# Every second row takes the low weights' product first: matmul order in the projections of an 18-sublayer stack

## The chip, the cores and the metric

The kernel runs on one core of one Trainium2 chip. The metric is the device time of one execution in microseconds (us). A kernel's time is the median of several executions. Differences of about half a per cent are the smallest that such a measurement of this kernel can tell from none.

## The reference

One sequence of 256 tokens with 1024 features passes through two blocks, of four layers and of two. Every layer is: half-weighted feed-forward sublayer, mixer sublayer, half-weighted feed-forward sublayer, each with an RMS norm before and after. That makes 18 sublayers: 12 feed-forward ones and 6 mixers (HGRN twice, differential attention, pooling, a hybrid of Mamba-2 and forgetting attention, RG-LRU). In short:

```python
def swiglu(x, w_in, w_out):
    g, u = jnp.split(x @ w_in, 2, axis=-1)        # 1024 -> 2 x 2816
    return (jax.nn.silu(g) * u) @ w_out           # 2816 -> 1024

for i in range(DEPTH):
    h = h + 0.5 * rmsnorm(swiglu(rmsnorm(h, gn[0]), ffn1_w_in[i], ffn1_w_out[i]), gn[1])
    m = mixer(rmsnorm(h, gn[2]))                  # starts with a projection x @ w_in, ends with one
    h = h + rmsnorm(m, gn[3])
    h = h + 0.5 * rmsnorm(swiglu(rmsnorm(h, gn[4]), ffn2_w_in[i], ffn2_w_out[i]), gn[5])
```

Everything is float32. The work is in the matrix products of the projections, the feed-forward ones above all.

## The kernel before

Activations are kept by feature: a tile has 128 features on the partitions and the 256 tokens (T) along the free dimension, so the 1024 features are KD = 8 rows k of such tiles. Weights come from HBM as panels of 1 MB (`raw`), 256 output columns wide and 8 rows deep; each goes into one of five slots.

**High and low parts.** TensorE multiplies the type fp32r, which is coarser than float32. So every weight panel is split by two engines. ScalarE rounds it to fp32r (`whi`, L1582), and VectorE subtracts (`wlo` = `raw` - `whi`, L1778, in place of `raw`). Activations are split the same way: `xs[:, k, 0:T]` holds the high part of row k and `xs[:, k, T:2T]` the low part beside it; `hs` is the same for the hidden layer of the feed-forward sublayers. A product of weights and activations is then three terms: high weights by high and by low activations, and low weights by high activations.

**One row of a tile's sum.** `tile_product` (L2010) makes the three terms with two matmuls. The high weights (128x128) are multiplied with the 512 columns of `x_k`, so that the first half of a PSUM bank gets high by high and the second half high by low (L2012). The low weights are multiplied with the 256 high columns and added to the first half of the bank (L2013). In this document H is the first kind of matmul (512 columns) and L the second (256 columns), and "a pair" is H and L of one row. Each matmul has a weight load of its own (the rows PEld). A tile of 128 outputs sums 8 rows in one bank: H L H L ..., sixteen matmuls; a panel has two tiles (`ft`). When the panel is done, ScalarE copies the second halves of the banks to `corr` (L1672), and VectorE adds them to the first halves (L1858).

**Where pairs of this kind run.** `in_product` (L2015) calls `tile_product` for the panels of the input projections (`panel_product`, L2079), 20 panels of each feed-forward sublayer and some of each mixer. `down_products` (L2114) calls it for the feed-forward output projection: first seven wide panels with all eight output tiles, two rows k each (L2123), then the last eight rows of every tile, tile by tile (L2133). Some tiles of the output projection use `summed_product` (L2004) in place of it: three matmuls of 256 columns each, high by high, high by low, low by high, all into the same half bank.

**The first two panels** of each sublayer take another path, `first_pair` (L2018): four tiles in turn for each row k, so that TensorE can start as soon as row k of the activations is there. From its second row on it takes the low weights of the four tiles first (L2037), and then the high weights of the four tiles (L2035): L L L L H H H H. The last two rows are made with two tiles at a time: L L H H.

**Order and queues.** Each engine has one program written out by hand, with semaphores between them. TensorE waits once a panel for the split weights (`weights_lo`) and for the banks (`panel_out`), and issues 32 matmuls behind that. The last matmul of a panel raises `panel_done`. Weight DMAs are issued by SyncE's queue, one per panel.

Of the kernel before, what the change touches and what calls it, by code (L numbers as in the profile page):

```python
# [2 lines left out]

# [1 line left out]

# [10 lines left out]
P = 128  # L16
T = 256
TT = T // P
D = 1024
KD = D // P  # L20
FF = 2816
KF = FF // P
PC = 256
SLOTS = 5
# [39 lines left out]
def build(nc, a, out):  # L64
# [9 lines left out]
    for l in range(4):  # L74
        g = VEC_GAIN1 + 6 * l
# [11 lines left out]
    for l in range(2):  # L87
        g = VEC_GAIN2 + 6 * l
# [38 lines left out]
    with ctx:  # L127
        def sb(name, shape, dt=F32):
            return ctx.enter_context(nc.sbuf_tensor(name, shape, dt))
# [3 lines left out]
        def sem(name):  # L133

            if name not in sems:
                sems[name] = ctx.enter_context(nc.semaphore(name))
            return sems[name]
# [5 lines left out]
        wlo = nc.alloc_sbuf_tensor_at("wlo", [P, SLOTS, PANEL], F32R, offset=raw_offset)  # L143
        whi = sb("whi", [P, SLOTS, PANEL], F32R)
# [41 lines left out]
        in_banks = (pp[:, 0:2, :], pp[:, 2:4, :])  # L186
# [1814 lines left out]
        def _(pe):  # L2001
            mm = nc.tensor.matmul
# [4 lines left out]
                mm(bank[:, 0:T], whi[:, slot, c:c + P], x_k[:, T:2 * T], start=False, stop=False)  # L2007
                return mm(bank[:, 0:T], wlo[:, slot, c:c + P], x_k[:, 0:T], start=False, stop=stop)  # L2008

            def tile_product(bank, slot, c, x_k, start, stop):  # L2010

                mm(bank, whi[:, slot, c:c + P], x_k, start=start, stop=False)  # L2012
                return mm(bank[:, 0:T], wlo[:, slot, c:c + P], x_k[:, 0:T], start=False, stop=stop)  # L2013

            def in_product(g, half, ft, x, k):  # L2015
                return tile_product(in_banks[half][:, ft, :], g % SLOTS, k * PC + ft * P, x[:, k, :], k == 0, k == KD - 1)

            def first_pair(seg, fill):  # L2018

# [59 lines left out]
            def panel_product(g, half, between=None):  # L2079
                pe.wait_ge(sem("weights_lo"), splits_before[g] + 1)  # L2080
                for ft in range(2):
                    for k in range(KD):
                        e = in_product(g, half, ft, xs, k)
                    if ft == 0 and between is not None:
                        between()
                e.then_inc(sem("panel_done"), 1)
# [27 lines left out]
            def down_products(s, wide_rows, last_rows, wide_wait, last_wait):  # L2114

                seg = s["segs"][-1]
                for p in range(seg.wide):
                    pe.wait_ge(sem("weights_lo"), splits_before[seg.g0 + p] + 1)
                    wide_wait(p)
                    for ft in range(KD):  # L2120
                        if p == 0 and ft in (4, 6):
                            pe.wait_ge(sem("panel_out"), seg.r0 - (ft == 4))
                        for k in range(2):  # L2123
                            product = summed_product if ft >= KD - 2 else tile_product
                            e = product(out_banks[ft // 2][:, ft % 2, :], (seg.g0 + p) % SLOTS, k * D + ft * P,
                                        hs[:, wide_rows[2 * p + k], :], p + k == 0, False)
                    e.then_inc(sem("panel_done"), 1)
                last_wait()
                for pair in range(4):
                    g = seg.g0 + seg.wide + pair  # L2130
                    pe.wait_ge(sem("weights_lo"), splits_before[g] + 1)
                    for ft in range(2):
                        for k in range(KD):  # L2133
                            product = summed_product if pair == 3 else tile_product
                            e = product(out_banks[pair][:, ft, :], g % SLOTS, k * PC + ft * P, hs[:, last_rows[k], :],
                                        False, k == KD - 1)
                        if pair == 3 and ft == 0:
                            e.then_inc(sem("last_tile_begun"), 1)
                            first_sums(s)
                    e.then_inc(sem("panel_done"), 1)  # L2140
                output_sums(s)
# [19 lines left out]
            def first_sums(s):  # L2161
                pe.wait_ge(sem("squares_added"), 3 * s["n"] + 2)
                mm(psum_stat, ones[:, :], sq[:, 0, :], start=True, stop=False)

            def output_sums(s):

                pe.wait_ge(sem("squares_added"), 3 * s["n"] + 3)
                mm(psum_stat, ones[:, :], sq[:, 4, :], start=False, stop=False)
                pe.wait_ge(sem("last_squares"), 2 * s["n"] + 2)
                mm(psum_stat, ones[:, :], sq[:, 7, :], start=False, stop=True).then_inc(sem("squares_summed"), 1)  # L2170
# [81 lines left out]
            for s in subs:  # L2252
                segs = s["segs"]
                if s["kind"] == FFN:
                    ffn_in(s)
                    f = s["ffn"] * (FF // PC)
                    down_products(s, range(14), range(14, KF), wide_wait=lambda w: pe.wait_ge(sem("hidden_lo"), f + w + 1),
                                  last_wait=lambda: pe.wait_ge(sem("hidden_lo"), f + FF // PC))
                else:
                    last = (out_begin, out_rows, long_out if s["kind"] == HYB else out_rest) if s["kind"] != REC else out_products  # L2260
                    PE_MIX[s["kind"]](pe, s, products, down_products, last, first_of, column_sums, keep_clock)
# [105 lines left out]
```

## Time and profile before

| | |
|---|---|
| median of 3 runs | 3162.26 us |
| lowest and highest | 3154.13 and 3171.62 us |
| span of the profiled execution | 3152.9 us |
| TensorE (PE) busy | 3104.0 us, 98% of the span, 18100 matmuls |
| TensorE weight load (PEld) busy | 2710.0 us, 86% |
| VectorE (DVE) busy | 2183.9 us, 69% |
| ScalarE (ACT) busy | 1681.8 us, 53% |
| GpSimd (POOL) busy | 4.0 us |
| bytes read from HBM | 530.99 MB, 169 GB/s over the span |
| mean granted TensorE clock | 0.998 of full speed |

The span runs from the first to the last instruction of one profiled execution. It is 9.4 us shorter than the median of the runs; that much is taken as what lies around it. PE busy time is the union of matmul intervals whose ends are modelled and overlap, so it tells that TensorE was never without work, not how fast the work went. The rate is read from the distance between the starts of successive matmuls.

### The profile page before, as it was taken

The page shows a single profiled execution, that of the slowest core. Times are in us where ns is not written, and L with a number is a line of the kernel's source. Part 1 is how long each engine was busy: PE and PEld are TensorE (multiplying, and loading weights), DVE is VectorE, ACT ScalarE, POOL GpSimd, SP SyncE. Part 2 cuts the span into 40 slices and gives each one's busy share as a digit, 9 for nine tenths or more (in the row PEclk, how much of TensorE's full clock was granted, in tenths as well). Part 3 has the DMA queues.
Part 4 walks back from the last instruction along what each step waited for, and adds up shares of the span by engine and source line. Part 5 has one row for each costly group of instructions (what it writes and reads, how often), then busy time and mean ns, then how long its engine had stood idle before and what let it go on. Part 6 is the DMA issues. An engine that isn't in the chain of part 4 may idle for free.

```text
span 3152.9 us, 44746 instructions
## 1 busy us (share of the span) xinstructions
PE 3104.0 (98%) x18100; PEld 2710.0 (86%) x18100; DVE 2183.9 (69%) x2635; ACT 1681.8 (53%) x2069; POOL 4.0 (0%) x22
## 2 busy tenths in 40 slices
PE   9999999999999999999999999999999999999998
PEld 8888888888888888888888888888888888888887
DVE  7768675867586775685867877585874675857674
ACT  6566654645464654454546665464642554545553
POOL 0000000000000000000000000000000000000000
PEclk9999999999999999999999999999999999999999
DMA  6543454554355454455454345455432454554453
GB/s 232 188 173 134 149 187 173 190 190 155 120 187 186 175 187 172 149 187 187 174 187 164 131 159 189 161 200 187 162 136 104 161 194 167 198 188 147 147 187 120
DMA packets 75356, 534.78 MB, mean 170 GB/s; under 512 B 8480, under 2 KB 8608, under 8 KB 10784
## 3 DMA queue, kind: packets, MB, share of 16 engines
q1 hardware_dynamic: 75168, 532.07, 46.7%
q8 instruction: 143, 2.34, 0.3%
q14 instruction: 45, 0.37, 0.0%
HBM read 530.99 MB, written 1.05 MB: 169 GB/s over the span
## 4 chain that ended last, share of the span: by engine, by line
PE 92%; DVE 4%; DVEq 2%; ACT 1%; issue 1%; DMA 0%; SPq 0%; ACTq 0%
PE pp L2012 36%; PE pp L2013 18%; PE pm L2012 8%; PE pp L2174 5%; PE pm L2013 4%; PE pp L2035 4%; PE pp L2007 2%; PE pp L2037 2%; PE pp L2006 2%; PE pp L2008 2%; PE pp L2065 2%; PE pp L2217 1%; PE pp L2075 1%; DVE wlo L1778 1%; DMA raw<-weights 0%
## 5 line engine op out<-in xcount | busy, mean ns | idle before, releaser
L2012 PE MATMUL pp<-xs,whi 128*128 128x512 f32 x4592 | 1615.7, 397 | 7.8 <-DVE tsum L1858 7.4
L1778 DVE TENSOR_TENSOR wlo<-raw,whi 128x2048 fp32r<-128x2048 f32 x461 | 1053.8, 2289 | 417.8 <-ACT whi L1582 417.3
L2013 PE MATMUL pp<-xs,wlo 128*128 128x256 f32 x4592 | 1283.2, 279 | 0.0
L2012 PEld LDWEIGHTS pp<-xs,whi 128*128 128x128 f32 x4592 | 861.0, 188 | 219.1 <-DVE tsum L1858 17.3
L1582 ACT ACTIVATE whi<-raw 128x2048 fp32r<-128x2048 f32 x461 | 879.5, 1911 | 281.4 <-DMA raw<-weights 280.7
L2013 PEld LDWEIGHTS pp<-xs,wlo 128*128 128x128 f32 x4592 | 866.1, 189 | 0.6
L1672 ACT ACTIVATE corr<-pp 128x512 f32<-128x512 f32 x335 | 199.5, 595 | 620.9 <-PE pp L2013 595.6
L1858 DVE TENSOR_TENSOR tsum<-pp,corr 128x512 f32<-128x512 f32 x323 | 222.4, 689 | 234.5 <-ACT corr L1672 234.3
L2012 PE MATMUL pm<-hs,whi 128*128 128x512 f32 x1056 | 377.2, 397 | 0.0
L2013 PE MATMUL pm<-hs,wlo 128*128 128x256 f32 x1056 | 296.7, 281 | 0.0
L2012 PEld LDWEIGHTS pm<-hs,whi 128*128 128x128 f32 x1056 | 198.9, 188 | 45.0
L2013 PEld LDWEIGHTS pm<-hs,wlo 128*128 128x128 f32 x1056 | 198.2, 188 | 0.0
L2012 PE MATMUL pp<-hs,whi 128*128 128x512 f32 x528 | 190.8, 397 | 0.0
L2035 PE MATMUL pp<-xs,whi 128*128 128x512 f32 x576 | 166.3, 400 | 16.1 <-DVE xs L1789 16.1
L2006 PE MATMUL pp<-hs,whi 128*128 128x256 f32 x528 | 150.5, 285 | 0.0
L2007 PE MATMUL pp<-hs,whi 128*128 128x256 f32 x528 | 148.4, 281 | 0.0
L2008 PE MATMUL pp<-hs,wlo 128*128 128x256 f32 x528 | 148.4, 281 | 0.0
L2013 PE MATMUL pp<-hs,wlo 128*128 128x256 f32 x528 | 148.4, 281 | 0.0
L1684 ACT ACTIVATE hs<-hid 128x512 fp32r<-128x512 f32 x132 | 83.5, 633 | 108.5 <-DVE hid L1874 108.4
L2174 PE MATMUL pp<-mix,raw 128*128 128x256 f32 x576 | 129.1, 383 | 2.5 <-DVE mix L358 2.5
L2174 PEld LDWEIGHTS pp<-mix,raw 128*128 128x128 f32 x576 | 109.8, 192 | 19.6 <-DVE mix L328 2.9
L2035 PEld LDWEIGHTS pp<-xs,whi 128*128 128x128 f32 x576 | 95.5, 188 | 33.4 <-issue 22.5
(350 smaller groups left out, 3166.2 us busy)
## 6 DMA issues: line engine op xcount, KB each, us to landing
raw<-weights SPq DMA_DIRECT2D x503, 1024.0 KB, 4.8
raw<-weights SPq DMA_DIRECT2D x8, 256.0 KB, 6.9
h<-x_by_feature SPq DMA_DIRECT2D x4, 256.0 KB, 6.2
out<-h SPq DMA_DIRECT2D x4, 256.0 KB, 2.5
vec<-vectors SPq DMA_DIRECT2D x1, 264.0 KB, 2.8
lamrow<-diff_lambda SPq DMA_DIRECT2D x1, 128.0 KB, 11.8
skiprow<-ssm_d SPq DMA_DIRECT2D x1, 8.0 KB, 12.0
```

The lines of the kernel that those rows point to most:

```text
L1582: nc.scalar.activation(whi[:, slot, :], raw[:, slot, :], ACT.Copy).then_inc(sem("weights_hi"), 1)
L1672: nc.scalar.activation(two(corr[:, half, :]), banks[:, :, T:2 * T], ACT.Copy).then_inc(sem("corr_copied"), 1)
L1684: nc.scalar.activation(hs[:, 2 * j:2 * j + 2, 0:T], two(hid[:, :]), ACT.Copy).then_inc(sem("hidden_hi"), 1)
L1778: v.tensor_tensor(wlo[:, slot, :], raw[:, slot, :], whi[:, slot, :].bitcast(F32), ALU.subtract).then_inc(sem("weights_lo"), 1)
L1858: v.tensor_tensor(to, banks[:, :, 0:T], two(corr[:, half, :]), ALU.add).then_inc(sem("panel_out"), 1)
L2006: mm(bank[:, 0:T], whi[:, slot, c:c + P], x_k[:, 0:T], start=start, stop=False)
L2007: mm(bank[:, 0:T], whi[:, slot, c:c + P], x_k[:, T:2 * T], start=False, stop=False)
L2008: return mm(bank[:, 0:T], wlo[:, slot, c:c + P], x_k[:, 0:T], start=False, stop=stop)
L2012: mm(bank, whi[:, slot, c:c + P], x_k, start=start, stop=False)
L2013: return mm(bank[:, 0:T], wlo[:, slot, c:c + P], x_k[:, 0:T], start=False, stop=stop)
L2035: e = mm(bank, whi[:, slot, c:c + P], xs[:, k, :], start=(k == 0), stop=(k == KD - 1))
L2174: return mm(in_banks[p % 2][:, ft, 0:T], raw[:, g % SLOTS, c:c + P], x[:, k, :], start=start, stop=stop)
```

## The change

`tile_product` gets an argument `low_first`. With it, the low weights' matmul is issued first and the high weights' matmul second; the last one issued carries `stop`. It is set for every row with odd k in the input projections, for the second of the two rows of a wide panel, and for odd rows among the last eight of the output projection. The first row of a tile stays high first, since its 512-column matmul opens the whole bank. `summed_product`, `first_pair` and all other matmuls are as before. The order of a tile goes from H L H L H L H L to H L L H H L L H, and since a tile ends with H and the next begins with H, the stream is L L H H L L H H throughout. The number, shapes, operands and results of the matmuls are the same; the terms of each sum are added in another order.

```diff
+from functools import partial
...
-            def tile_product(bank, slot, c, x_k, start, stop):
-
+            def tile_product(bank, slot, c, x_k, start, stop, low_first=False):
+
+                if low_first:
+                    mm(bank[:, 0:T], wlo[:, slot, c:c + P], x_k[:, 0:T], start=False, stop=False)
+                    return mm(bank, whi[:, slot, c:c + P], x_k, start=False, stop=stop)
                 mm(bank, whi[:, slot, c:c + P], x_k, start=start, stop=False)
                 return mm(bank[:, 0:T], wlo[:, slot, c:c + P], x_k[:, 0:T], start=False, stop=stop)
...
-                return tile_product(in_banks[half][:, ft, :], g % SLOTS, k * PC + ft * P, x[:, k, :], k == 0, k == KD - 1)
+                return tile_product(in_banks[half][:, ft, :], g % SLOTS, k * PC + ft * P, x[:, k, :], k == 0, k == KD - 1, k % 2 == 1)
...
-                            product = summed_product if ft >= KD - 2 else tile_product
+                            product = summed_product if ft >= KD - 2 else partial(tile_product, low_first=k == 1)
...
-                            product = summed_product if pair == 3 else tile_product
+                            product = summed_product if pair == 3 else partial(tile_product, low_first=k % 2 == 1)
```

## Rows read from the trace of the kernel before

**Rows 1.** The page: engines and clock, then the chain that ended last, by line.
```profile
PE 3104.0 (98%) x18100; PEld 2710.0 (86%) x18100; DVE 2183.9 (69%) x2635; ACT 1681.8 (53%) x2069; POOL 4.0 (0%) x22
...
PEclk9999999999999999999999999999999999999999
...
PE 92%; DVE 4%; DVEq 2%; ACT 1%; issue 1%; DMA 0%; SPq 0%; ACTq 0%
PE pp L2012 36%; PE pp L2013 18%; PE pm L2012 8%; PE pp L2174 5%; PE pm L2013 4%; PE pp L2035 4%; PE pp L2007 2%; PE pp L2037 2%; PE pp L2006 2%; PE pp L2008 2%; PE pp L2065 2%; PE pp L2217 1%; PE pp L2075 1%; DVE wlo L1778 1%; DMA raw<-weights 0%
```
**Rows 2.** PE's waits: engine, line, waited for: us in total, times, longest.
```profile
PE pp L2035 <- DVE xs L1789: 16.1, 17, 1.0
PE pp L2012 <- DVE tsum L1858: 7.4, 8, 2.1
```
**Rows 3.** Groups by line: operation, tiles, shapes, count | busy us, mean ns | idle before.
```profile
L2012 PE MATMUL pp<-xs,whi 128*128 128x512 f32 x4592 | 1615.7, 397 | 7.8 <-DVE tsum L1858 7.4
L2012 PE MATMUL pm<-hs,whi 128*128 128x512 f32 x1056 | 377.2, 397 | 0.0
L2012 PE MATMUL pp<-hs,whi 128*128 128x512 f32 x528 | 190.8, 397 | 0.0
```
**Rows 4.** L2012 alone, 90 us of feed-forward inputs: us, busy (count), clock, DMA, GB/s.
```profile
31.00:121.00 90.00, 90.00 (x260) 48.63 (x260) 1.00 0.53 194
372.00:462.00 90.00, 90.00 (x256) 47.91 (x255) 1.00 0.51 185
...
2975.00:3065.00 90.00, 90.00 (x256) 47.92 (x255) 1.00 0.52 185
```
**Rows 5.** L2012 alone between the starts of two of its matmuls, first stage.
```profile
39.58:118.62 79.04, 79.04 (x229) 42.75 (x229) 1.00 0.52 188
```
**Rows 6.** Timeline of PE, first feed-forward stage: start us, us, line, operation.
```profile
39.93 0.39 PE L2012 MATMUL pp<-xs,whi 128*128 128x512 f32 x1
40.16 0.27 PE L2013 MATMUL pp<-xs,wlo 128*128 128x256 f32 x1
40.27 0.40 PE L2012 MATMUL pp<-xs,whi 128*128 128x512 f32 x1
...
40.97 0.40 PE L2012 MATMUL pp<-xs,whi 128*128 128x512 f32 x1
```
**Rows 7.** Timeline of PE, second feed-forward sublayer's input stage.
```profile
382.01 0.40 PE L2012 MATMUL pp<-xs,whi 128*128 128x512 f32 x1
...
384.13 0.40 PE L2012 MATMUL pp<-xs,whi 128*128 128x512 f32 x1
```
**Rows 8.** Timeline of PE, output projection: pairs, then the three 256-column matmuls.
```profile
145.17 0.40 PE L2012 MATMUL pm<-hs,whi 128*128 128x512 f32 x1
...
147.29 0.40 PE L2012 MATMUL pm<-hs,whi 128*128 128x512 f32 x1
...
149.06 0.28 PE L2006 MATMUL pp<-hs,whi 128*128 128x256 f32 x1
...
149.41 0.28 PE L2006 MATMUL pp<-hs,whi 128*128 128x256 f32 x1
```
**Rows 9.** Timeline of PE, first_pair of a feed-forward sublayer, LLLLHHHH and then LLHH.
```profile
547.23 1.08 PE L2035 MATMUL pp<-xs,whi 128*128 128x512 f32 x4
...
548.62 1.09 PE L2035 MATMUL pp<-xs,whi 128*128 128x512 f32 x4
...
551.43 1.09 PE L2035 MATMUL pp<-xs,whi 128*128 128x512 f32 x4
552.36 0.40 PE L2037 MATMUL pp<-xs,wlo 128*128 128x256 f32 x2
552.60 0.63 PE L2035 MATMUL pp<-xs,whi 128*128 128x512 f32 x2
553.06 0.40 PE L2037 MATMUL pp<-xs,wlo 128*128 128x256 f32 x2
...
554.46 0.39 PE L2037 MATMUL pp<-xs,wlo 128*128 128x256 f32 x2
```

## The prediction

> **What bounds the kernel now.** I read the page first. TensorE is busy for 98% of the span, its granted clock is 9 tenths or more in every slice, which is its 2.4 GHz level, and the chain of work that ended last lies for 92% on TensorE; lines 2012 and 2013, the two that the change reorders, hold 66% of the span in it (36 + 18 + 8 + 4) [rows 1]. Then the waits: TensorE's longest total against one releaser is 16.1 us, in `first_pair`, which the change leaves alone, and the next is 7.4 us [rows 2]. So nothing that TensorE waits for is worth much; what counts is how fast it streams one matmul after another.
>
> How fast is not in the mean durations, since their ends are modelled: the mean of 397 ns for H [rows 3] is longer than the distance from one H to the next. I take starts. In the first feed-forward stage H begins at 39.93, its L at 40.16 and the next H at 40.27: about 230 ns for H, 115 for L; three pairs take 1.04 us [rows 6]. Over a long stretch it is exact: 229 starts of L2012 from 39.58 to 118.62, so 228 pairs in 79.04 us, 346.7 ns a pair [rows 5]. In the next feed-forward sublayer six pairs take 384.13 - 382.01 = 2.12 us, 353.3 ns a pair [rows 7]. Nothing in the code differs between the two. Windows of 90 us in all twelve feed-forward input stages show just these two rates: 260 or 261 starts in eight of them, 256 in four [rows 4]. I call them the quick rhythm and the slow rhythm. In the output projection six pairs take 147.29 - 145.17 = 2.12 us, the slow rhythm again, and there three matmuls of 256 columns take 149.41 - 149.06 = 0.35 us [rows 8]. That last row matters: H and L are 768 columns with two weight loads, the three are 768 columns with three weight loads and no 512-column matmul among them, and both take 353 ns. Time goes by columns, not by the number of loads or by what stands next to what.
>
> **What the change removes, adds and moves.** It removes and adds no matmul, load, wait or transfer. It reorders the two matmuls in every second row. The pairs are 4592 + 1056 + 528 = 6176 [rows 3]; half of them, 3088, are turned round, and the stream becomes L L H H. Nobody is released earlier or later within a tile: the last matmul of a panel is now H, which starts 115 ns sooner than L did, and ends when L ended, since the same columns stand before that point. The waits on `weights_lo`, `panel_out` and `hidden_lo` stand ahead of the first matmul of a panel and keep their place, and SP's queue isn't touched. So the whole question is what a pair costs in the order L L H H.
>
> The trace of before shows that very order, in the last two rows of `first_pair`. There the blocks L L H H begin at 552.36, 553.06, with two more up to 554.46: three blocks, six pairs, in 2.10 us, 350 ns a pair. Its middle rows, L L L L H H H H, begin an H block at 547.23 and at 551.43, three turns of four pairs later: 4.20 / 12 = 350 ns again [rows 9]. Two L together took 0.24 us and two H 0.46 us. So 350 ns is my price. It differs from the stream at hand in one way: there neighbours of one kind share the activations of one row, here they don't. The ends around it are the two rhythms, 346.7 and 353.3 ns.
>
> The sum, in terms of pairs:
> - eight quick feed-forward stages, 20 panels of 16 pairs each: 8 x 320 = 2560 pairs, from 346.7 to 350, +3.3 ns each: +8.5 us (0 to +17.1 between the ends);
> - four slow stages, 4 x 320 = 1280 pairs, from 353.3 to 350: -4.3 us (-8.5 to 0);
> - the mixers' projections, 4592 - 3840 = 752 pairs, in short stretches that I put at the middle of the two rates: 0 (-2.5 to +2.5);
> - the output projections, 1056 + 528 = 1584 pairs at 353.3. Two different makeups took the same time there, which speaks for 0; the price of 350 would give -5.3 us, the quick rhythm -10.5. I take half of the former: -2.6 us.
>
> Together +8.5 - 4.3 + 0 - 2.6 = +1.6 us on a span of 3152.9. The median of the runs is 9.4 us above that span, and I carry this over: 3162.26 + 1.6 = 3164 us. The ends are 0 - 8.5 - 2.5 - 10.5 = -21.5 us, all in the quick rhythm, and +17.1 + 2.5 = +19.6 us, all in the slow one. The three runs of before lie 17.5 us apart, which is what eight stages cost between the rhythms (17.1 us); the trace of one execution can't show whether that is the cause.
>
> A rule of the Trainium skill bears on this. First the row: L lasts some 115 ns from start to start and holds the load for the next matmul under it, and an L that follows an L costs no visible excess, 0.24 us for two [rows 9]. "TensorE: Matmul & The Clock Gate", section "LDWEIGHTS (loading the stationary operand)", gives a load of 128 columns as P / 1.2, 107 ns, and its section on the back-to-back gap gives 109 ns for a warm matmul of 256 columns. By that rule a load just fits under an L in either order, and the sum would be zero; but it leaves 2 ns of slack, so a load only slightly slower would make L L the bad order. The same section's gaps for 512 and 256 columns add to 325 ns for a pair; the trace disagrees, with 346.7 and 353.3.
>
> **The rivals.**
> *All quick (faster).* Alternating H and L might be what throws the stream into the slow rhythm: each H is followed by something of another length. If blocks of two of a kind keep it quick everywhere, the time is 3162.26 - 21.5 = 3141 us, -0.7%. For it: the switch between the rhythms has no visible cause in the code, so it hangs on something as small as order. Against it: the L L H H of `first_pair` took 350 and not 346.7.
> *Uncovered load (slower).* While H streams, the queue has 115 ns to spare beside the load of L. If that slack is now used to get ahead with the load after it, then in L L H H the second L has no such stock, and its load sticks out. The place is the matmul behind the first L of each block. The dearest that the rows allow there is what two L took above twice 115: 0.24 - 0.23 = 0.01 us, give or take as much for the two decimals, so 0 to 20 ns; it decides from about 5 ns, where 3088 x 5 = 15 us. At a middle 7 ns it gives 3088 x 7 = 21.6 us, 3184 us. Against it: three loads under three 256-column matmuls cost no more than two loads in a pair [rows 8].
> *All slow.* If blocks of unlike activations lose the quick rhythm for good, the price is +19.6 us, 3182 us. Its nearest row is the 353.3 of the slow stages.
> *The change does nothing.* The array might be bound by columns alone, with the rhythm set by how each stage starts. The time is then 3162 us, with stages falling into one or the other as they do now.
>
> **How the numbers follow.** My forecast of 3164 us, with prices of 348 to 352 ns, has 0.45; that the order does nothing, 0.13; all quick 0.20; all slow 0.10; uncovered load 0.12. Half a per cent is 16 us, about what a measurement of this kernel can tell from no change. The first two lie within it: 0.58. All quick is faster: 0.20. All slow and uncovered load are slower: 0.22. The range runs from the bound of all quick, a little beyond it at 3139, to 3184, the middle of the uncovered load, and leaves out the rest of both: gains from blocks that beat even the quick rhythm, and loads that stick out by 10 ns or more. The likeliest case's own range is 3152 to 3172.
>
> **What the profile after would show.** The count of L2012's successor in 90 us windows of the twelve stages: near 258 in all if my price is right, 260 or 261 if all are quick, 256 if all are slow, under 253 if loads stick out. Starts: blocks of 0.70 us; the second L of a block at 0.12 us behind the first, and more than that if its load is uncovered. The waits of TensorE should stay within some 2 us of [rows 2]. I am wrong if the output projection's pairs move by more than 4 ns from 353, or if any block takes less than 0.69 us: then the order of unlike matmuls has a price of its own, which I have put at nearly nothing.

## The result

The changed kernel takes 3139.87 us (median of 4, 3139.15 to 3141.14), the kernel before 3162.74 us beside it (median of 4, 3154.13 to 3171.62). The ratio is 0.9923, 95% interval 0.9902 to 0.9943: faster by 0.8%, where 3164 us and no change beyond half a per cent had been forecast. Two things stand out. The time is within 2 us of the rival "all quick" (3141 us), though the trace does not bear its mechanism out in the input stages. And the executions of the changed kernel lie within 2 us of each other, where those of the kernel before were 17.5 us apart.

The page after, with the lines that answer to [rows 1], then TensorE's two longest waits by releaser, as in [rows 2]:

```profile
PE 3089.7 (98%) x18100; PEld 2700.5 (86%) x18100; DVE 2185.3 (70%) x2635; ACT 1681.6 (54%) x2069; POOL 4.1 (0%) x22
...
PE 91%; DVE 5%; DVEq 2%; ACT 1%; issue 1%; DMA 0%; POOL 0%; POOLq 0%; ACTq 0%; SPq 0%
...
PE pp L2039 <- DVE xs L1790: 16.2, 17, 1.0
PE pp L2016 <- DVE tsum L1859: 6.9, 7, 2.1
```

The waits are the same to 0.5 us, VectorE and ScalarE work as long as before, and TensorE's busy time is 14.3 us shorter, just as the span is (3138.6 against 3152.9 us). The gain lies in the stream itself.

To compare rates I take windows that begin just behind the start of one matmul and end as far behind the start of the matmul 224 pairs later, in the dense part of an input stage; the columns are stretch, its length, busy (count of matmuls that read `xs`), granted clock, share of the DMA engines, GB/s. First the kernel before, stages 1, 2 and 12 of the twelve:

```profile
36.51:114.17 77.66, 77.66 (x450) 1.00 0.52 190
377.82:456.96 79.14, 79.14 (x450) 1.00 0.50 185
...
2980.51:3059.65 79.14, 79.14 (x450) 1.00 0.52 186
```

Then the changed kernel, the same three:

```profile
36.89:114.91 78.02, 78.02 (x450) 1.00 0.54 189
377.46:455.49 78.03, 78.03 (x450) 1.00 0.54 189
...
2968.84:3046.86 78.02, 78.02 (x450) 1.00 0.53 189
```

Before: 77.66 / 224 = 346.7 ns a pair in eight stages and 79.14 / 224 = 353.3 ns in four. After: 78.02 / 224 = 348.3 ns in all twelve, a new rate between the two, not the quick one. The same view for the last rows of the output projection, over 40 pairs, with `hs`; first before, then after:

```profile
173.14:187.27 14.13, 14.13 (x82) 1.00 0.55 176
```

```profile
173.40:187.26 13.86, 13.86 (x82) 1.00 0.50 183
```

That is 353.3 ns a pair before and 346.5 ns after, in all twelve output projections. Since 13.86 us is read to 0.01, the rate after lies between 346.3 and 346.7; by the trace's whole nanoseconds, two pairs begin 693 or 694 ns behind the two before once the stretch is under way, and that is 346.7 ns, the quick rhythm. The timeline of the changed kernel shows how the new order runs there (start us, us, line; L2016 and L2015 are H of even and odd rows, L2017 and L2014 their L), to be held against [rows 8]:

```profile
145.95 0.40 PE L2016 MATMUL pm<-hs,whi 128*128 128x512 f32 x1
146.19 0.28 PE L2017 MATMUL pm<-hs,wlo 128*128 128x256 f32 x1
146.31 0.28 PE L2014 MATMUL pm<-hs,wlo 128*128 128x256 f32 x1
146.42 0.39 PE L2015 MATMUL pm<-hs,whi 128*128 128x512 f32 x1
146.65 0.40 PE L2016 MATMUL pm<-hs,whi 128*128 128x512 f32 x1
```

An H behind which another H waits takes 0.23 us to the next start, one behind which an L waits takes 0.24, and the second L of the two takes 0.11, the first 0.12. The block H L L H takes 0.69 us (2 x 346.5 ns) where two pairs took 0.71.

The account between the two profiled executions: the output projections give 1584 x (353.3 - 346.5) = 10.8 us; the eight quick input stages lose 2560 x (348.3 - 346.7) = 4.1 us; the four at the slow rhythm give 1280 x (353.3 - 348.3) = 6.4 us. Together 13.1 of the 14.3 us; the other 1.2 us are left to the mixers' 752 pairs, and start to start over every such pair of the two traces the mixers' do come out 1.3 us shorter. The medians moved by more, 22.9 us. The difference is in the kernel before: the profiled execution of the changed kernel took 3140.28 us as a run, 1.7 us above its span, so 1.7 and not 9.4 us lie around a span. The profiled execution of before took 3152.9 + 1.7 = 3154.6 us by that, one of the faster ones of its kernel, whose median of the first four executions stands 8 us above it. In 46 later executions of the kernel before, beside the experiments, the median is 3157 to 3158 us, so part of the 22.9 us is that the first four came out high; five more executions of the changed kernel, beside 17 of those, are 16.8 us faster.

### The profile page after: what moved, and what is told of

Same layout as the page of the kernel before. It is cut to its first block, busy times and chain, and to the rows that moved or that the text cites. A ratio compares the mean times of both kernels' runs of the same rounds, so it can differ in the third digit from the quotient of the medians.

```text
span 3138.6 us, 44746 instructions
## 1 busy us (share of the span) xinstructions
PE 3089.7 (98%) x18100; PEld 2700.5 (86%) x18100; DVE 2185.3 (70%) x2635; ACT 1681.6 (54%) x2069; POOL 4.1 (0%) x22
## 4 chain that ended last, share of the span: by engine, by line
PE 91%; DVE 5%; DVEq 2%; ACT 1%; issue 1%; DMA 0%; POOL 0%; POOLq 0%; ACTq 0%; SPq 0%
PE pp L2016 18%; PE pp L2015 18%; PE pp L2017 9%; PE pp L2014 9%; PE pp L2178 5%; PE pp L2039 4%; PE pm L2016 4%; PE pm L2015 4%; PE pp L2041 2%; PE pm L2017 2%; PE pp L2009 2%; PE pp L2007 2%; PE pm L2014 2%; PE pp L2008 2%; PE pp L2069 2%; PE pp L2221 1%
## 5 line engine op out<-in xcount | busy, mean ns | idle before, releaser
L2016 PE MATMUL pp<-xs,whi 128*128 128x512 f32 x2296 | 916.2, 399 | 7.2 <-DVE tsum L1859 6.9
L2015 PE MATMUL pp<-xs,whi 128*128 128x512 f32 x2296 | 908.3, 396 | 0.0
L2014 PE MATMUL pp<-xs,wlo 128*128 128x256 f32 x2296 | 639.2, 278 | 0.0
L2017 PE MATMUL pp<-xs,wlo 128*128 128x256 f32 x2296 | 636.9, 277 | 0.0
L2014 PEld LDWEIGHTS pp<-xs,wlo 128*128 128x128 f32 x2296 | 431.0, 188 | 104.8
L2017 PEld LDWEIGHTS pp<-xs,wlo 128*128 128x128 f32 x2296 | 431.8, 188 | 96.6
L2016 PEld LDWEIGHTS pp<-xs,whi 128*128 128x128 f32 x2296 | 435.9, 190 | 19.4 <-DVE tsum L1859 16.8
L2015 PEld LDWEIGHTS pp<-xs,whi 128*128 128x128 f32 x2296 | 430.3, 187 | 0.0
L2016 PE MATMUL pm<-hs,whi 128*128 128x512 f32 x528 | 209.6, 397 | 0.0
L2015 PE MATMUL pm<-hs,whi 128*128 128x512 f32 x528 | 205.0, 388 | 0.0
L2039 PE MATMUL pp<-xs,whi 128*128 128x512 f32 x576 | 166.2, 400 | 16.2 <-DVE xs L1790 16.2
L2017 PE MATMUL pm<-hs,wlo 128*128 128x256 f32 x528 | 148.2, 281 | 0.0
L2009 PE MATMUL pp<-hs,wlo 128*128 128x256 f32 x528 | 147.9, 280 | 0.0
L2014 PE MATMUL pm<-hs,wlo 128*128 128x256 f32 x528 | 145.9, 276 | 0.0
```

Of the source, the lines that this page charges most:

```text
L2015: return mm(bank, whi[:, slot, c:c + P], x_k, start=False, stop=stop)
L2039: e = mm(bank, whi[:, slot, c:c + P], xs[:, k, :], start=(k == 0), stop=(k == KD - 1))
```

## The experiments

The theory after the result, called A: the stream of matmuls has its own price for each order, H L H L falls by chance into one of two rhythms in every input stage of every execution, and H L L H has one rhythm only. Against it stood B: the two halves of the change work on each other, the rhythm of one stage being handed to the next. The place of the operands in SBUF, the traffic of other engines and the weight loads were the suspects for where the price comes from.

### The change in the output projections only

```diff
-                return tile_product(..., k == 0, k == KD - 1, k % 2 == 1)
+                return tile_product(..., k == 0, k == KD - 1)
```

> The new order only in the output projections (`down_products`); the input projections keep H L H L. Theory A (each order has a price of its own, and the H L stream of the input stages falls by chance into a quick or a slow rhythm in each execution): the output projections give 1584 pairs x 7.3 ns = 11.5 us, so the median is near 3151 us against 3162 us for the kernel before, and the scatter between executions (17 us in the kernel before) stays, since it comes from the input stages. In the profile, twelve input stages at 346.7 or 353.6 ns a pair. Theory B (the change as a whole keeps the stream quick, since a slow output projection throws the next sublayer's stages out of step): all input stages are quick here too, the scatter is gone, and the time is near 3136 us.

Measured: 3145.12 us (median of 12, 3140.41 to 3154.58), ratio 0.9956 (0.9935 to 0.9977) to the kernel before, whose 29 executions beside it have a median of 3158.05 us. The input stages kept both rates; here stages 2 and 3:

```profile
376.38:454.03 77.65, 77.65 (x449) 1.00 0.54 189
565.74:644.88 79.14, 79.14 (x449) 1.00 0.53 186
```

Five of the twelve are slow in this execution, and the scatter stayed (14 us). So making the output projections quick doesn't make the input stages quick, and B falls in this form. The gain of 12.9 us is near the 10.8 us of the account and the 11.5 us of theory A. Of the 29 executions of the kernel before, 28 lie within 10.4 us; the other, at a mean granted clock of 0.935 where they had 0.997 to 0.999, took 3193.53 us.

### The change in the input projections only

```diff
-                            product = summed_product if ft >= KD - 2 else partial(tile_product, low_first=k == 1)
+                            product = summed_product if ft >= KD - 2 else tile_product
...
-                            product = summed_product if pair == 3 else partial(tile_product, low_first=k % 2 == 1)
+                            product = summed_product if pair == 3 else tile_product
```

> The new order only in the input projections; the output projections keep H L H L. Theory A: all twelve input stages at 348.4 ns a pair, the scatter between executions falls from 17 us to about 2 us, the output projections stay at 353.4 ns, and the median is 11.5 us above that of the changed kernel, near 3151 us. Theory B: the input stages, entered from slow output projections, show two rates from stage to stage, and the scatter stays.

Measured: 3151.70 us (median of 12, 3149.68 to 3153.53), ratio 0.9973 (0.9953 to 0.9993). All twelve input stages run at 78.02 / 224 = 348.3 ns and all output projections at 353.4 ns; the scatter is 3.9 us. Both are as A expected, the scatter somewhat wider than its 2 us.

### Both halves again

No edit: the changed kernel.

> The changed kernel itself, beside the kernels of this call on the same chip, as the sum of the two halves. If the halves add up (output projections alone 0.9956, input projections alone 0.9973 of the kernel before), it is at 0.9929 of the kernel before, and its executions lie within 3 us of each other. If the halves overlap, it is above 0.994.

Measured: 3140.12 us (median of 5, 3137.42 to 3140.47), ratio 0.9942 (0.9927 to 0.9956) to 17 executions of the kernel before with a median of 3156.90 us. The two halves together, 0.9956 x 0.9973 = 0.9929, lie within that interval, at its edge. The ratio itself is just above 0.994, where the expectation had put an overlap. So this run can't tell halves that add up from a small overlap; that they add up is told by the rates, which are the same in each half alone and in both together (348.3 ns and 346.5 ns). The gain is somewhat smaller than in the first comparison since the kernel before came out at 3157 to 3158 us here, and at 3163 us in its first four executions.

### The kernel before, two more executions with a profile

> The kernel before, unchanged, in another execution with a profile: does the number of slow input stages tell its time? In the profile of before four of twelve were slow (353.8 against 346.6 ns a pair, 2.3 us a stage). If the rhythm is the cause of the scatter, an execution with n slow stages takes about 3154 + 2.3 x (n - 4) us, give or take 2 us for the mixers' stages, which have rhythms too. If the scatter has another cause, time and count don't go together.

> The same once more: another execution of the kernel before, with 3154 + 2.3 x (n - 4) us for n slow input stages if the rhythm makes the scatter.

Measured: 3146.73 us with one slow stage of twelve (the second), 3152.14 us with four (the first four); forecast by the rule, 3147.1 and 3154. Stages 1 and 2 of the first execution, then stages 4 and 5 of the second:

```profile
36.77:114.42 77.65, 77.65 (x450) 1.00 0.53 189
378.18:457.32 79.14, 79.14 (x450) 1.00 0.52 187
```

```profile
891.13:970.27 79.14, 79.14 (x450) 1.00 0.52 186
1083.12:1160.77 77.65, 77.65 (x450) 1.00 0.53 189
```

The same program, bit for bit, has its stages in another rhythm in each execution, and between these two the time follows their number: three more slow stages cost 5.4 us, that is 1.8 us each, where 320 x (353.3 - 346.7) = 2.1 us are due. Start to start in the traces, the twelve input stages differ by 6.3 us, which is 2.1 for each of the three; the rest of the execution gave 0.9 us back. The earlier profiled execution had four stages in the slow rhythm too and a span 2.5 us longer than this one with four (3152.9 against 3150.4 us), so something besides varies as well. It isn't the mixers' pairs, which took 1.2 us less there. Some 1.7 us of it are one stretch of another matmul, L390, near the end: first the earlier execution, where the granted clock was 0.59 from 2892 to 2896 us, then this one:

```profile
2892.16 4.54 PE L390 MATMUL pm<-mix,raw 128*128 128x256 f32 x12 [1.70 <-DVE small L298]
```

```profile
2893.53 2.86 PE L390 MATMUL pm<-mix,raw 128*128 128x256 f32 x12 [1.70 <-DVE small L298]
```

From 3146.7 us with one slow stage, a median of 3158 us would have six or seven slow stages at 2.1 or 1.8 us each. That is an estimate: no execution near the median has a profile, and neither have the slowest ones.

### TensorE alone

A kernel of its own, which loads three weight panels and the input and then does nothing but run streams of matmuls, 12 tiles of 8 rows each. It leaves out the whole computation of the reference. One of its streams:

```diff
+            for n in range(4):
+                mm(pm[:, 3, 0:240 if n == 3 else T], ones[:, :], keep[:, 0:240 if n == 3 else T], start=True, stop=True)
+            for tile in range(12):
+                for i, (w, k) in enumerate(orders("HL")):
+                    bank, lhs, rhs = place(tile, w, k, "lo", 0, False)
+                    mm(bank, lhs, rhs, start=(i == 0), stop=(i == len(orders("HL")) - 1))
```

> Nothing of the reference is computed: the output is zeros. After loading three weight panels and the input, TensorE alone runs 25 streams, each of 96 pairs (12 tiles of 8 rows) or what the order makes of them, with no transfer and no other engine at work; 3 matmuls of 256 columns and one shorter or equal one of type float32 stand between streams, to shift the start. Orders: H L; H L L H; runs of 4 and of 8 of a kind; H alone; L alone; three 256-column matmuls per row; low first in every row; the weights of L taken from `whi`; one row of activations only; one weight address only; each with the activations at a multiple of 128 bytes, some also 16, 32 and 64 bytes past it. Theory A (price of an order, rhythm by start): H L at 0 bytes shows 346.7 and 353.4 ns in its four starts, H L L H 348.4 ns at each start and 346 ns at 64 bytes. Theory C (the excess over 325 ns, and the two rhythms, come from the other engines' and the DMAs' traffic in SBUF): all streams run near 325 ns, whatever the order. Theory D (the address of the weights decides): the streams with one weight address or one weight source differ from the others by several ns a pair.

The windows run over the 72 rows from the third tile to the eleventh, with the same columns as above. In this order: H L at 0 bytes with a 256-column start, and with a 240-column start; H L at 64 bytes, both starts; H L L H at 0 bytes; H L L H at 64 bytes; three matmuls of 256 columns at 0 bytes, and at 64 bytes.

```profile
29.21:54.65 25.44, 25.44 (x146) 1.00 0.00 1
64.73:89.69 24.96, 24.96 (x146) 1.00 0.00 1
169.49:194.61 25.12, 25.12 (x147) 1.00 0.01 1
204.74:230.18 25.44, 25.44 (x146) 1.00 0.00 1
240.33:265.41 25.08, 25.08 (x146) 1.00 0.00 1
310.53:335.37 24.84, 24.84 (x146) 1.00 0.00 1
547.39:573.31 25.92, 25.92 (x218) 1.00 0.01 1
583.57:609.01 25.44, 25.44 (x218) 1.00 0.01 1
```

Per row: H L at 0 bytes 353.3 and 346.7 ns, H L at 64 bytes 348.9 and 353.3, H L L H 348.3 at 0 bytes and 345.0 at 64, the three matmuls 360.0 at 0 bytes and 353.3 at 64. With no transfer under way and no other engine at work, the rates of the real kernel are there to the tenth of a nanosecond: 346.7, 353.3 and 348.3 ns in the input stages, 353.3 in the old output projections and for their three-matmul tiles. One isn't: the new output projections run at 346.5 to 346.7 ns, and the stream like them at 345.0; no run shows why. Theory C is refuted: the rhythms are there with TensorE alone. The output projections of the kernel before are the streams at 64 bytes: `hs` begins 64 bytes past a multiple of 128, `xs` at a multiple.

The other streams: runs of four of a kind 350.8 ns and of eight 349.2 ns at 0 bytes, and of eight 344.9 ns at 64 bytes, so more neighbours of one kind don't help; low first in every row 349.9 ns, mostly an alternation again; L reading its weights from `whi`, one row of activations only, or one weight address only, 346.7 ns each, a rate that H L shows anyway, so none of these is needed for it. With one stream each, they can't settle theory D. H alone took 226.7 ns and L alone 120.0 ns, together 346.7.

### More starts and more places

The same kernel with other streams.

> Nothing of the reference is computed: the output is zeros. Streams on TensorE alone, as in the streams before, 12 tiles of 8 rows each. Eight streams of H L with the activations at a multiple of 128 bytes that differ only in the length of the float32 matmul ahead of them (256, 256, 240, 208, 176, 144, 112, 80 columns); one behind a stream of 256-column matmuls; three starts of H L at 64 bytes; H L L H at 0, 16, 32, 48, 64, 80, 96 and 112 bytes and at other starts; three 256-column matmuls per row at 0, 16, 32 and 64 bytes; the same with every second row turned round. Theory A with the rhythm set by the start: H L falls to 346.7 or to 353 ns from start to start, and H L L H has one rate at each place, 348.4 at 0 and 345.0 at 64 bytes, whatever stands ahead. If the rhythm is not set by the start, all eight streams of H L agree. The three 256-column matmuls should take 360 ns a row at 0 bytes and 353.4 at 64.

In this order: H L at 0 bytes, twice with the same 256-column start; three matmuls of 256 columns at 0 bytes; H L at 64 bytes; H L L H at 0, and at 64 bytes.

```profile
29.27:54.23 24.96, 24.96 (x146) 1.00 0.00 1
64.37:89.81 25.44, 25.44 (x146) 1.00 0.00 1
312.52:338.44 25.92, 25.92 (x218) 1.00 0.01 1
454.85:480.29 25.44, 25.44 (x146) 1.00 0.01 1
525.84:550.92 25.08, 25.08 (x146) 1.00 0.00 1
666.48:691.32 24.84, 24.84 (x146) 1.00 0.00 1
```

The first two streams are the same instructions, and one is quick, the other slow. Of the eight starts of H L at 0 bytes six were slow (353.3) and two quick (346.7), and a ninth, behind the stream of three matmuls, was quick; in the kernel of streams above, one of four was slow. The first stream of both kernels is the same, with the same matmuls ahead, and was slow there and quick here. H L at 64 bytes was slow in all three starts. H L L H gave 348.3 ns in both starts at 0 bytes and 345.0 in all three at 64 bytes. Other places: 348.3 at 16 bytes, 346.7 at 32, 350.0 at 48, 80 and 96, 348.9 at 112. Turning every second row of the three-matmul form round changed nothing (360.0 and 353.3). The expectation held on each point. So the length of the matmul ahead does not decide the rhythm.

### The weight load's share

> Nothing of the reference is computed: the output is zeros. Streams on TensorE alone again. The weights are 128, 64 or 32 columns wide, so that their load is shorter; the moving columns stay 512 and 256. The weights' address is moved by 32 and by 64 bytes with the activations at 0 and at 64. H L has four starts each with the activations at 32 and at 16 bytes. Theory X (the excess over 325 ns a pair comes from the weight load, which shares something with the moving operand): with half the load it halves or vanishes, and the weights' address matters as much as the activations' does. Theory M (the excess is in reading the moving operand alone): 348.4 and 345.0 ns for H L L H at 0 and 64 bytes whatever the width and the address of the weights.

With weights of 64 columns in place of 128, H L took 340.0 ns at 0 bytes and 343.3 at 64; with 32 columns 348.3 at both. H L L H took 350.0 and 347.8 ns with 64 columns, 346.7 and 350.0 with 32. The excess that theory X has in mind doesn't halve with half the load, and with a quarter of it is as large as ever, against theory X; but it doesn't stay put either, against theory M. The weights' address counts as well: moved by 64 bytes together with the activations (both at 64), H L L H took some 349 ns in place of 345.0 (moved by 32 bytes, 351.5 with the activations at 0 and 347.2 at 64), and the three-matmul form with the weights alone moved took 353.8 in place of 360.0. (One row in sixteen, at the panel's end, kept its weights' place.) So the places of both operands matter. It isn't their distance alone: with the weights moved by 64 bytes and the activations at 0, H L L H took 347.9 ns, not the 345.0 of the opposite case. The windows, again over 72 rows: H L L H with the weights moved, the activations at 0 and at 64; the three-matmul form with the weights moved; H L with weights of 64 columns at 0 bytes.

```profile
557.37:582.42 25.05, 25.05 (x145) 1.00 0.00 1
592.53:617.64 25.11, 25.11 (x145) 1.00 0.00 1
627.63:653.10 25.47, 25.47 (x218) 1.00 0.01 1
273.89:298.37 24.48, 24.48 (x145) 1.00 0.00 1
```

H L with the activations at 16 or 32 bytes was quick in all four starts each. How load and moving operand meet in the engine stays open.

### Moving the activations of the kernel before

```diff
+        sb("mix_pad", [P, 16])
         mix_offset = nc.sbuf_base
...
```

> The kernel before with 64 bytes of padding ahead of `mix` and `hs`, so that `hs` begins at a multiple of 128 bytes as `xs` does; in the kernel before it begins 64 bytes past one. No order is changed. Theory A1 (the slow 353.4 ns of the output projections comes from where their activations lie in SBUF): they go to the two rates of the input stages, 346.7 ns where they are quick, and the median falls by up to 1584 x 6.7 = 10.6 us, to about 3152 us. Theory A2 (place has nothing to do with it, order alone has a price): the output projections stay at 353.4 ns and the time stays at 3162 us within the scatter.

Measured: 3148.73 us (median of 12, 3145.60 to 3151.02), ratio 0.9964 (0.9944 to 0.9984). The time fell by 9.3 us, which A2 had not said. The median is near what A1 said, and its reason is wrong: the output projections stayed at 353.3 ns, as A2 said, and it was the input stages that were quick, all twelve of them in the profiled execution. The three-matmul tiles went from 0.35 to 0.36 us a row, as in the streams at 0 bytes. Why the input stages should be quick more often when `hs`, which they don't read, is moved, no run shows. That what comes ahead of a stage sways its rhythm is a guess; the order of the rows in the output projection did not. But the odds of the two rhythms are not the same in every layout, and "by chance" in theory A has to be read with that.

Next, `xs` of the kernel before is moved by 64 bytes:

```diff
+        sb("xs_pad", [P, 16])
...
         xs = sb("xs", [P, KD, 2 * T], F32R)
+        sb("after_pad", [P, 16])
```

> The kernel before with `xs` moved by 64 bytes in the same way; the order stays H L H L. Theory A: the input stages run at the two rates that H L showed 64 bytes past a multiple of 128, 348.9 and 353.1 ns, in place of 346.7 and 353.8 ns. The sum for each stage of 320 pairs is between +0.7 us (quick to quick) and -0.2 us (slow to slow), so the median stays within 6 us of the kernel before, and the scatter between executions shrinks from 17 us, since the two rates lie closer together. Theory A2: stages at 346.7 and 353.8 ns as before.

Measured: 3166.03 us (median of 12, 3162.09 to 3171.16), ratio 1.0029 (1.0020 to 1.0038). Eleven input stages at 353.3 ns, one at 348.9, the two rates of the streams. The time is 9 us above the kernel before, not within 6: the rates were foreseen, and that the slower of them would nearly always win was not.

### Moving the activations of the changed kernel

The same edit on the changed kernel.

> The changed kernel with `xs` moved by 64 bytes, so that it begins 64 bytes past a multiple of 128 as `hs` does; all else lies where it was. Theory A (the price of H L L H depends on where the activations lie: 348.4 ns at a multiple of 128 bytes, 345.0 ns 64 bytes past it): the twelve input stages go from 348.4 to 345.0 ns, 3840 x 3.4 = 13.1 us, and with the mixers' part of it the time is 13 to 16 us below the changed kernel. Theory A2 (place has no part in it): no change from the changed kernel, within 2 us.

Measured: 3123.57 us (median of 4, 3120.16 to 3124.41), ratio 0.9888 (0.9871 to 0.9905), 16.6 us below the changed kernel beside it (3140.12 us). Input stages 1 and 2, then 40 pairs of an output projection:

```profile
37.13:114.41 77.28, 77.28 (x450) 1.00 0.53 191
375.46:452.74 77.28, 77.28 (x450) 1.00 0.54 191
```

```profile
172.61:186.41 13.80, 13.80 (x82) 1.00 0.50 180
```

All twelve input stages at 345.0 ns, and the output projections at 345.0 too. Twelve stages give 3840 x 3.3 = 12.7 us and the output projections 1584 x 1.5 = 2.4 us, 15.1 of the 16.6 us. The second part had not been expected: the two pads leave `hs` 64 bytes past a multiple of 128, where it was, but 128 bytes further on. So H L L H at 64 bytes has two rates too: 346.5 to 346.7 ns in all twelve output projections of the changed kernel, and of the version with the change in the output projections only, and 345.0 ns in all twelve here and in five streams. No run shows what chooses between them. Moving `xs` by 64 bytes is worth nearly as much as the change, and only together with it: on the old order it cost 9 us. This version is the fastest of all.

## Why the prediction was wrong

**What bounds the kernel** was right: TensorE's rate of streaming and nothing else. Waits, transfers and the other engines did not move.

**The input stages' price** was nearly right, and the term still changed its sign. Six pairs of `first_pair` in the order L L H H [rows 9] gave 350 ns, and the stream took 348.3. The error of 1.7 ns over 3840 pairs is 6.5 us: the term was put at +4.2 us and came out at -2.3 us. Two starts read to 0.01 us give 2.10 / 6 no better than to 1.7 ns, so the rows could not have told the sign of this term. And the rows differed from the stream in more than the prediction said: in `first_pair` neighbours of one kind also go to different banks.

**The output projections' term** is the one that failed most: 8.2 of the 15.9 us between the forecast (+1.6 us) and the change of the span (-14.3 us). It was put at -2.6 us and measured -10.8 us. The step behind it: three 256-column matmuls and a pair both took 353 ns [rows 8], therefore time goes by columns and order costs nothing there. That was a coincidence of one place. At 0 bytes the same two forms take 360.0 and 346.7 or 353.3 ns. The price of 350 was then carried over from `xs` to `hs` and halved, though nothing in the rows said that two buffers have the same price; H L L H costs 348.3 ns in one and 345.0 to 346.7 in the other. The prediction's own sign of being wrong came true here: these pairs moved by 6.8 ns, more than the 4 it had allowed, so the order has a price of its own. Its other sign, a block of less than 0.69 us, was just missed.

**The link from span to median** was wrong by 8 us. The 9.4 us between the span and the median were taken as lying around the execution; only 1.7 us do. The rest is that the profiled execution was a fast one. That the median has more slow stages than its four is the likely reason and isn't shown, since no execution near the median has a profile; and 4 to 6 of the 8 us are that the first executions came out above the 3157 to 3158 us of the later ones. The prediction had noted that the scatter of 17.5 us is what eight stages cost between the rhythms, and had not drawn the consequence, which is that a change that fixes the rhythm must be costed against the mean of the rhythms over executions and not against those of one. Against the later medians, only 2 to 4 us of the gain come by that way.

**The rivals.** "All quick" gave 3141 us and had 0.20. That its time came out is luck: it took 21.5 us off, where the span fell by 14.3, and the slow first executions of the kernel before made up for the rest. Its mechanism was half right. The output projections gained 10.8 us where it had 10.5, and at 0 bytes it is H L H L that lets the stream fall into a slow rhythm; but no input stage is at 346.7 ns, the eight quick ones lost 4.1 us, and it had them lose nothing. "Uncovered load" is refuted by starts: the second L begins 0.12 us behind the first, as the prediction had it for a load that is covered, and the H behind it 0.11 us later. The rule of the Trainium skill weighed with it ("TensorE: Matmul & The Clock Gate", section "Back-to-back issue gap") gives gaps of 512 and 256 columns that add to 325 ns in any order. The trace disagrees: the streams give 345.0 to 353.3 ns for a pair at full clock, 6 to 9% more, and different rates for different orders. "All slow" and "does nothing" are out: all twelve input stages went to 348.3 ns.

**The range** ended at 3139 and the time was 3139.87, inside it; what was wrong is the forecast of no change, at 0.58, and its direction.

## What to carry to other kernels

Where TensorE is never idle, the distance between starts is the thing to read, and it should be read in more than one stage and more than one execution: equal code at two rates is a finding, not noise. A stream of matmuls of unlike lengths can have two steady rates, and a pattern of another period can remove the bad one; try the order and the operands' place in SBUF together, since the place that gained 16.6 us with the new order cost 9 us with the old one. A kernel of streams on TensorE alone costs one execution, showed all rates of the real kernel here but one, and tells the price of an order before it is built in.

## What the hardware showed

At a granted clock of 1.00, the 2.4 GHz level, and with nothing else running, a pair of 512 and 256 fp32r columns, with weights of 128 columns, took 345.0 to 353.3 ns according to order, start and place; three matmuls of 256 columns took 350.0 ns a row with the activations 32 bytes past a multiple of 128, 353.3 at 64, 356.0 at 16 and 360.0 at 0. The same 192 instructions ran at 346.7 ns a pair in one stream and at 353.3 in the next. Alone, H took 226.7 ns at 0 bytes and 228.9 at 64, L 120.0 and 117.8: what is good for the one is bad for the other. And the scatter of an execution's time, 17.5 us in the kernel before's first four executions and 10 to 12 us in later ones, fell to 2 to 4 us with H L L H in the input stages. That it was for the most part TensorE's choice of rhythm is borne out by the two executions whose slow stages were counted, not shown for the whole of it.
